# A hybrid attention, DeltaNet and MoE step: the 16x16 blocks of the DeltaNet scan turned on VectorE, planes in DRAM moved by half, triangles written by the sync queue

## Chip, cores and metric

The kernel runs on one core of a Trainium2 chip. The metric is the device time of one execution in microseconds. Three runs of the kernel before took 2502.2, 2504.52 and 2506.75 us: median 2504.52. Everything is float32.

## The reference

One trunk layer runs over 256 context tokens and 1024 latent tokens (D = 1024): a modulated input projection, two token mixers side by side (grouped-query attention, and a gated DeltaNet in both directions), their merge, and a hierarchical mixture of experts. The change touches the DeltaNet scan alone. For 8 heads of 64 channels, two directions and chunks of 64 tokens it computes

```python
lmat = jnp.where(strict, jnp.einsum('bhnik,bhnjk->bhnij', k_beta, k) * decay, 0.0)
tmat = lax.linalg.triangular_solve(eye + lmat, jnp.broadcast_to(eye, lmat.shape),
                                   left_side=True, lower=True, unit_diagonal=True)
u = jnp.einsum('bhnij,bhnjv->bhniv', tmat, v_beta)
w = jnp.einsum('bhnij,bhnjk->bhnik', tmat, k_beta * jnp.exp(g)[..., None])
intra = jnp.where(incl, jnp.einsum('bhnik,bhnjk->bhnij', q, k) * decay, 0.0)
def step(S, xs):                                   # one chunk after the other
    v_new = u_c - jnp.einsum('bhck,bhkv->bhcv', w_c, S)
    o_c = jnp.einsum('bhck,bhkv->bhcv', q_c, S) + jnp.einsum('bhij,bhjv->bhiv', a_c, v_new)
    S = S * jnp.exp(gl_c)[..., None, None] + jnp.einsum('bhck,bhcv->bhkv', k_c, v_new)
```

For every chunk, head and direction a unit triangular 64x64 matrix has to be inverted.

## The kernel before

The kernel is one program for five engines with hand-written semaphores; between its stages all engines meet. The fourth stage is the scan. There are 20 chunks, 4 of context and 16 of latent tokens. Iteration s handles chunk s of the forward direction together with the matching chunk of the backward direction, so 16 matrices of 64x64 at once. They lie on the 128 partitions as two halves (h) of 64 rows, with eight matrices side by side (a = 4 d + p: direction d, pair of heads p).

The engines run in their own order through the same loop, from s = -4 to 20 (AHEAD = 4). In iteration s they prepare chunk n = s + 4 (decays, Gram products, masked triangles la) and finish chunk s (inverse, new values, state, outputs).

The inverse is built in levels. First all 16x16 diagonal blocks are inverted by substitution, for two chunks at a time: 2 chunks x 16 matrices x 4 blocks = 128 blocks, one per partition. This is base(b) on VectorE for the chunks 2b and 2b+1, in iteration n = 2b + 2, an even s: rows 1 to 7 behind L1703, rows 8 to 15 at the end of the iteration behind L1726. Each row is a product (L1661) and a negated sum (L1664), each waited for before the next. The blocks are then doubled twice on TensorE with masks (the products x4, t4, u4 and x5, u5; the masks at L1678, the subtractions at L1701, L1703 and L1726 on VectorE).

To bring the blocks onto one partition each, and the inverses back into 64x64 planes, the data go through DRAM:

- GpSimd writes the triangle of chunk n - 1 from la to lt_scratch, one DMA per direction and half (L2039), behind its own work of the iteration.
- SP reads the diagonal blocks, one DMA per direction (L569), into b_turn (forward) and b_in (backward). Blocks of the backward direction are upper triangles, so ScalarE turns them (L1296) from b_in to b_turn.
- VectorE substitutes. The result is b_inv. Both the inverse and its transpose are needed; ScalarE turns all of it into b_invt (L1319), at the end of its iteration.
- SP writes b_inv and b_invt to tu_scratch (L551: two chunks x two directions x two forms, eight DMAs), waits until they have landed, and reads 64x64 planes into tu (L559: two chunks x two forms x two directions x two halves, sixteen DMAs). The parts off the diagonal blocks were zeroed once, at the start of the program. After that it reads the next blocks.

A plane in DRAM is 64x64 + 64 elements, so that consecutive diagonal blocks lie 16 x 64 + 16 elements apart over matrices and chunks alike.

On TensorE an iteration is: x4 (waits for tu and for the mask of the iteration before); the decay products (L923, L924); kv and av of chunk s - 1 (wait for ScalarE's copy L1280 of the new values); t4 (waits for L1678) and u4; two products with constants; x5; the product with the state; the Gram products (L953); u5; the product of the state with the queries; vn. All but L923, L924 and L953 are issued at L900: 32 small matmuls each, 16 matrices in two passes. On VectorE the order is: mask L1678, state L1698, L1701, L1703, outputs, base(b, 1, 8) if even, mask L1678, triangles L1722, L1726, base(b, 8, 16) if even. On ScalarE: L1280, eight exponentials L1285, L1290, the turn L1296, eight copies L1303, L1307, L1313, the turn L1319.

Of the kernel before, what the change touches and what calls it, by code (L numbers as in the profile page):

```python
# [22 lines left out]
P = 128  # L23
# [8 lines left out]
C = 64  # L32
# [13 lines left out]
def shape_constants():  # L46

    part, free = np.arange(P), np.arange(P)
    half, t = part // C, part % C
    same = (half[:, None] == half[None, :]).astype(np.float32)  # L50
    j = np.arange(C)
    upto = [t[:, None] <= j[None, :], t[:, None] >= j[None, :]]
    after_bd = [(t[:, None] > t[None, :]) * same, (t[:, None] < t[None, :]) * same]
    level = []
    for l in LEVELS:
        for d in range(2):
            b = 1 << l
# [11 lines left out]
    parts = [np.eye(P), same, np.ones((P, P))] + upto + after_bd + level + [eye, -eye, rot, before]  # L69
    return np.concatenate([np.asarray(a, np.float32) for a in parts], axis=1)  # L70
# [21 lines left out]
def build(nc, a, outs):  # L92
    ctx = ExitStack()
    with ctx:
# [21 lines left out]
        tu_d = nc.dram_tensor("tu_scratch", [4, 2, P, 16 * PLANE // P], F32).ap()  # L116
# [13 lines left out]
        eye_st, neg_eye, rot, before = take(C), take(C), take(P), take(P)  # L130
# [3 lines left out]
        def small_row(n):  # L134
# [49 lines left out]
          gm_ready decay_mm e_ready gr_ready e_masked el_ready kd_ready qd_ready gram_mm la_ready lt_out bt_in bt_turned  # L184
          base_done base_turned tu_out x4_mm x4_ready t4_mm t4_ready u4_mm u4_ready x5_mm x5_ready u5_mm u5_ready
# [151 lines left out]
        b_in, b_turn, b_inv, b_invt = [scr(256, "R1").rearrange("p (r c) -> p r c", r=16) for _ in range(4)]  # L337
# [17 lines left out]
        def planes_of(x, n, d, h):  # L355
            return bass.AP(x.tensor, (16 * n + 8 * d + 4 * h) * PLANE, [[C, C], [PLANE, 4], [1, C]])
# [91 lines left out]
        def _(sp):  # L448
# [86 lines left out]
            def blocks_of(x, n, d):  # L535
                return bass.AP(x.tensor, (16 * n + 8 * d) * PLANE, [[16 * C + 16, 32], [C, 16], [1, 16]])

            def block_rows(s, d):
                o = C * d + 32 * (s % 2)
                return slice(o, o + 32)  # L540
# [20 lines left out]
            for s in range(NCK):  # L561
                sp.wait_ge(S["lt_out"], 64 * (s + 1))
                if s % 2 == 0 and s > 0:
                    inverses_back(s // 2 - 1)
                if s // 2 > 0:
                    sp.wait_ge(S["base_done"], s // 2)
                    sp.wait_ge(S["bt_turned"], s // 2)
                for d in range(2):
                    sp.dma_start((b_turn, b_in)[d][block_rows(s, d)], blocks_of(lt_d, s, d)).then_inc(S["bt_in"], 16)  # L569
                if s == CTX_CH + 2:  # L570
# [4 lines left out]
            inverses_back(NCK // 2 - 1)  # L575
# [92 lines left out]
        def _(pe):  # L668
# [237 lines left out]
            for s in range(-AHEAD, NCK + 1):  # L906
# [5 lines left out]
                if now:  # L912
                    pe.wait_ge(S[f"tu_in{s % 3}"], landed(s, 3, 8))
# [208 lines left out]
        def _(act):  # L1122
# [152 lines left out]
            for s in range(-AHEAD, NCK + 1):  # L1275
# [15 lines left out]
                if n >= 2 and n % 2 == 0 and n // 2 - 1 < NCK // 2:  # L1291
                    b = n // 2 - 1
                    act.wait_ge(S["bt_in"], 64 * (b + 1))
                    if b > 0:
                        act.wait_ge(S["base_done"], b)
                    f(b_turn[C:2 * C].rearrange("p r c -> p c r"), b_in[C:2 * C], ACT.Copy).then_inc(S["bt_turned"], 1)  # L1296
# [17 lines left out]
                if n >= 2 and n % 2 == 0 and n // 2 - 1 < NCK // 2:  # L1314
                    b = n // 2 - 1
# [109 lines left out]
        def _(dve):  # L1425
# [233 lines left out]
            def substitute(b, i):  # L1659
# [3 lines left out]
                signal = "base_done" if i == 15 else "dve_chain"  # L1663
                v.tensor_reduce(b_inv[:, i, 0:i], tmp, AX.X, ALU.add, negate=True).then_inc(S[signal], 1)  # L1664
                dve.wait_ge(S[signal], count(signal))

            def base(b, first, end):
                if first == 1:
                    dve.wait_ge(S["bt_in"], 64 * (b + 1))
                    dve.wait_ge(S["bt_turned"], b + 1)  # L1670
                    if b > 0:
                        dve.wait_ge(S["base_turned"], b)
                        dve.wait_ge(S["tu_out"], 128 * b)
                for i in range(first, end):
                    substitute(b, i)

# [4 lines left out]
            for s in range(-AHEAD, NCK + 1):  # L1681
# [34 lines left out]
                if new:  # L1716
                    dve.wait_ge(S["gram_mm"], n + 1)
                    dve.wait_ge(S["e_masked"], n + 1)
                    if s > 0:
                        dve.wait_ge(S["av_mm"], s)  # L1720
                        dve.wait_ge(S["lt_out"], 64 * s)
# [230 lines left out]
        def _(pool):  # L1952
# [28 lines left out]
            for i in range(4):  # L1981
                for x in range(2):
                    pool.dma_start(tu_d[i, x], zero_f).then_inc(S["pool_dma"], 16)
# [40 lines left out]
            for s in range(-AHEAD, NCK):  # L2024
# [8 lines left out]
                if 1 <= n <= NCK:  # L2033
                    pool.wait_ge(S["la_ready"], n)
                    if n - 1 > 0:
                        pool.wait_ge(S["lt_out"], 64 * (n - 1))
                    for d in range(2):
                        for h in range(2):
                            pool.dma_start(planes_of(lt_d, n - 1, d, h), la[(n - 1) % RING][h * C:(h + 1) * C, 1, 4 * d:4 * d + 4]).then_inc(S["lt_out"], 16)  # L2039
# [77 lines left out]
```

## Time and profile before

| | before |
|---|---|
| median of three runs | 2504.52 us |
| the profiled execution | 2506.25 us |
| its span, first to last instruction | 2504.3 us |
| mean granted TensorE clock | 0.928 of full |
| TensorE busy (share of the span) | 2159.4 us (86%) |
| VectorE, ScalarE, GpSimd busy | 906.5, 682.8, 266.2 us |
| the scan in it | about 799 to 1236 us |

The span is about 2 us shorter than the time of the execution. The profile's page gives busy time by engine, the span in 40 slices, the chain that ended last and the costliest groups of instructions; a wait is written as the waiting instruction, an arrow and what ended the wait. The page's chain follows the end of the program and begins behind the scan, at 1326 us, so the scan has to be read from its own stretch: what ended the waits, and the engines' instructions in order of time. Numbers in brackets at the end of a line of the timeline are the idle time ahead of it and what ended it.

### The profile page before, as it was taken

Reading aid. Unit: us, or ns where it says so; the run is one execution under the profiler, and the core shown is the slowest. Engines: PE = TensorE matmul, PEld = TensorE weight load, DVE = VectorE, ACT = ScalarE, POOL = GpSimd, SP = SyncE. Lnnn points to the kernel's source line nnn. Section 1 sums busy time; section 2 is a strip of 40 time slices with the busy share of each in tenths; the row PEclk is TensorE's granted clock in tenths of the full one; section 3 lists DMA queues with packets and bytes.
Section 4 is the critical chain, followed back from the end, with each engine's and each line's share of the span. In section 5 each row is a group of like instructions: output and inputs, shape, how many; then the busy total and the mean of one; then the engine's idle time right before and its main releaser. Section 6 shows DMA issues by size and latency. Waiting matters only on the chain. (4 is left out here: it accounts for less than half of the span.)

```text
span 2504.3 us, 39485 instructions
## 1 busy us (share of the span) xinstructions
PE 2159.4 (86%) x16431; PEld 1329.9 (53%) x16431; DVE 906.5 (36%) x1760; ACT 682.8 (27%) x1386; POOL 266.2 (11%) x381
## 2 busy tenths in 40 slices
PE   4987999989997587888897999999999699799960
PEld 3545676665553477877753555555455444344420
DVE  3254666634883355455551011010223300000116
ACT  6122666643441232332220000000111122122223
POOL 2000000000000444433100000000000000000013
PEclk8998999999998698999898999999999699999985
DMA  9324000010100232323203111120313455776225
GB/s 331 130 88 121 4 4 1 2 43 26 30 0 1 43 63 46 62 43 58 57 0 92 26 34 43 25 67 1 136 60 117 150 185 179 250 239 214 85 101 201
DMA packets 240544, 210.12 MB, mean 84 GB/s; under 512 B 130348, under 2 KB 202352, under 8 KB 239728
## 3 DMA queue, kind: packets, MB, share of 16 engines
q1 hardware_dynamic: 223632, 152.93, 20.5%
q0 software_dynamic: 11696, 36.31, 4.9%
q10 hardware_dynamic: 5040, 18.35, 1.8%
q8 instruction: 133, 2.18, 0.4%
q14 instruction: 43, 0.35, 0.0%
HBM read 165.37 MB, written 42.01 MB: 83 GB/s over the span
## 5 line engine op out<-in xcount | busy, mean ns | idle before, releaser
L741 PE MATMUL ps<-R 128*128 128x512 f32 (+1 forms) x816 | 301.2, 530 | 11.3 <-SPq L525 8.4
L1008 PE MATMUL ps<-R 128*128 128x512 f32 (+1 forms) x768 | 286.1, 526 | 19.9 <-DMA R<-in_w_dn_br_dram 17.8
L1084 PE MATMUL ps<-R 128*128 x560 | 260.1, 619 | 25.7 <-SPq L653 22.5
L900 PE MATMUL ps<-R 64*64 64x64 f32 x5120 | 181.7, 230 | 67.8 <-ACT R L1280 30.5
L741 PEld LDWEIGHTS ps<-R 128*128 128x128 f32 x816 | 158.6, 195 | 150.7 <-issue 132.8
L1008 PEld LDWEIGHTS ps<-R 128*128 128x128 f32 x768 | 147.2, 192 | 152.3 <-issue 144.9
L900 PEld LDWEIGHTS ps<-R 64*64 64x64 f32 x5120 | 172.0, 145 | 87.4 <-ACT R L1280 37.4
L1084 PEld LDWEIGHTS ps<-R 128*128 128x128 f32 x560 | 110.7, 199 | 169.6 <-issue 169.6
L1753 DVE TENSOR_TENSOR R<-ps,R 128x512 f32<-128x512 f32 (+1 forms) x48 | 28.9, 603 | 394.1 <-ACT R L1353 393.3
L1920 DVE COPY R<-ps 128x256 f32<-128x256 f32 x35 | 14.9, 425 | 383.4 <-PE ps L1109 383.4
L2071 POOL DMA_INDIRECT R<-h_scratch,slot_i x35 | 33.0, 942 | 1124.6 <-DVE slot_i L1903 749.6
L1535 DVE TENSOR_SCALAR_CACHE_REDUCE R<-ps 128x512 f32<-128x512 f32 (+1 forms) x208 | 128.4, 666 | 59.9 <-PE ps L826 59.8
L1030 PE MATMUL ps<-R 128*128 128x512 f32 x320 | 142.2, 604 | 3.9 <-PEq L1017 3.9
L1010 PE MATMUL ps<-R 128*128 128x512 f32 (+1 forms) x384 | 145.3, 521 | 0.0
L1353 ACT ACTIVATE R<-ps 128x512 f32<-128x512 f32 (+1 forms) x48 | 25.2, 526 | 412.4 <-PE ps L1010 411.6
L1094 PE MATMUL ps<-R 128*128 x280 | 127.7, 599 | 1.5 <-DVE R L1920 1.3
L845 PEld LDWEIGHTS ps<-cst,R 128*128 128x128 f32 x800 | 86.4, 142 | 58.9 <-issue 48.2
L845 PE MATMUL ps<-cst,R 128*128 128x128 f32 x800 | 105.0, 279 | 5.7 <-ACT R L1239 2.9
L826 PE MATMUL ps<-R 64*128 64x512 f32 (+1 forms) x416 | 106.5, 616 | 3.5 <-SPq L509 3.3
L1229 ACT ACTIVATE R<-R 128x1536 f32<-128x1536 f32 (+1 forms) x80 | 108.6, 1358 | 3.0 <-DVE R L1544 2.9
L1010 PEld LDWEIGHTS ps<-R 128*128 128x128 f32 x384 | 73.0, 190 | 64.5 <-issue 61.2
L1030 PEld LDWEIGHTS ps<-R 128*128 128x128 f32 x320 | 61.2, 194 | 78.6 <-issue 73.9
(265 smaller groups left out, 2700.0 us busy)
## 6 DMA issues: line engine op xcount, KB each, us to landing
R<-in_w_mod_dram SPq DMA_DIRECT2D x12, 2048.0 KB, 9.1
slot_output<-R ACTq DMA_DIRECT2D x35, 512.0 KB, 3.6
R<-in_w_gate_e_dram SPq DMA_DIRECT2D x16, 1024.0 KB, 6.8
R<-in_w_up_e_dram SPq DMA_DIRECT2D x16, 1024.0 KB, 10.2
R<-in_w_down_e_dram SPq DMA_DIRECT2D x16, 1024.0 KB, 12.0
R<-in_w_in_dram SPq DMA_DIRECT2D x30, 512.0 KB, 5.4
R<-tu_scratch SPq DMA_DIRECT2D x160, 64.0 KB, 2.6
R<-in_x_sample_dram SPq DMA_DIRECT2D x16, 512.0 KB, 6.0
```

The costliest lines, as they stand in the source:

```text
L741: last = mm(ps[:, u % 4, 0:w], w_sb[n % NW][:, k, :], hT[:, k, c0:c0 + w], start=(k == 0), stop=(k == KD - 1))
L826: last = mm(ps[:, 2 * (u % 2) + g, 0:w], qT[lo, h4, qt * P:(qt + 1) * P], kT[lo, c0 + j * 512:c0 + j * 512 + w], start=True, stop=True)
L845: last = turn128(ps[:, 4 + v % 3, k * P:(k + 1) * P], s_sb[i % 2][g][:, j * 512 + k * P:j * 512 + (k + 1) * P], ident)
L900: last = mm(ps[lo, bank, a * C:(a + 1) * C], lhs(a)[lo], rhs(a)[lo], start=start and (alone or a == 0), stop=stop and (alone or a == PAIRS ...
L1008: mm(ps[:, o + x, 0:w], wk[:, x, k, :], hT[:, k, c0:c0 + w], start=(k == 0), stop=(k == KD - 1))
L1010: last = mm(ps[:, o + 2 + x, 0:w], wb[:, x, k, :], (aoT, odT)[x][:, k, c0:c0 + w], start=(k == 0), stop=(k == 3))
L1030: last = mm(ps[:, 2 * (n % 2) + h, :], mT[:, k, n * P:(n + 1) * P], ow[k][:, h * 512:(h + 1) * 512], start=(k == 0), stop=(k == KD - 1))
L1084: last = mm(ps[:, 2 + t % 2, :], hsT[t % 2][:, k, :], R[:, bass.ds(at + (RB + k * 512), 512)], start=(k == 0), stop=(k == KD - 1))
L1094: last = mm(ps[:, 5 + u % 3, :], hidT[t % 2][:, k, :], R[:, bass.ds(at + (RB + 4096 + k * D + h * 512), 512)], start=(k == 0), stop=(k == 1))
L1229: f(s_sb[i % 2][g][:, 0:w], s_sb[i % 2][g][:, 0:w], ACT.Exp, bias=shift[i % 2][g], accum_out=sums[qt % 2][:, g, h4:h4 + 1]).then_inc(S["p_ ...
L1535: v.tensor_scalar(s_sb[i % 2][g][:, j * 512:j * 512 + w], ps[:, 2 * (u % 2) + g, 0:w], HD ** -0.5, None, ALU.mult, ALU.max, accum_out=tops ...
L2071: pool.indirect_dma_start(hs[t % 2], None, h2_d, bass.IndirectOffsetOnAxis(ap=slot_i[:, t:t + 1], axis=0)).then_inc(S[f"hs_in{t % 2}"], 16)
```

## The change

It does five things.

1. Planes in DRAM are addressed by half, not by direction and half: planes_of takes eight planes at once. A chunk's inverses come back in four DMAs, a pair's in eight. blocks_of covers the blocks of two chunks on 128 partitions: one DMA reads them all into b_in, and one per form writes them. The order of tu_scratch changes to form first, then chunk, so that two chunks lie side by side.
2. With this order the direction of a block is bit 4 of its partition. A constant of two columns, block_dir, holds 1 for one direction and 0 for the other. VectorE makes b_turn as b_in times one mask plus turned b_in times the other, and after the substitution b_t and b_u in the same way from b_inv: six instructions per pair.
3. ScalarE's two turns and their semaphores are gone. base_done is now signalled by the last of the new instructions.
4. b_t uses the memory of b_in.
5. GpSimd's writes of the triangles are gone. SP does them, two DMAs per chunk, as soon as the triangle is ready: the one of an odd chunk after the loads of the pair before, the one of an even chunk after the read of the blocks and before the inverses are waited for.

```diff
-        def planes_of(x, n, d, h):
-            return bass.AP(x.tensor, (16 * n + 8 * d + 4 * h) * PLANE, [[C, C], [PLANE, 4], [1, C]])
+        def planes_of(x, n, h):
+            return bass.AP(x.tensor, (16 * n + 8 * h) * PLANE, [[C, C], [PLANE, 8], [1, C]])
+
+        def blocks_of(x, n):
+            return bass.AP(x.tensor, 16 * n * PLANE, [[16 * C + 16, P], [C, 16], [1, 16]])
...
             def inverses_back(b):
                 sp.wait_ge(S["base_done"], b + 1)
-                sp.wait_ge(S["base_turned"], b + 1)
                 for s in (2 * b, 2 * b + 1):
                     if s - 4 >= 0:
-                        sp.wait_ge(S[f"tu_in{(s - 4) % 3}"], landed(s - 4, 3, 8))
-                    for d in range(2):
-                        for x in range(2):
-                            src = b_inv if x == d else b_invt
-                            sp.dma_start(blocks_of(tu_d, 2 * (s % 4) + x, d), src[block_rows(s, d)]).then_inc(S["tu_out"], 16)
-                sp.wait_ge(S["tu_out"], 128 * (b + 1))
+                        sp.wait_ge(S[f"tu_in{(s - 4) % 3}"], landed(s - 4, 3, 4))
+                for x, src in enumerate((b_t, b_u)):
+                    sp.dma_start(blocks_of(tu_d, 4 * x + 2 * (b % 2)), src).then_inc(S["tu_out"], 16)
+                sp.wait_ge(S["tu_out"], 32 * (b + 1))
                 for s in (2 * b, 2 * b + 1):
                     if s - 2 > 0:
                         sp.wait_ge(S["vn_mm"], s - 2)
                     for x in range(2):
-                        for d in range(2):
-                            for h in range(2):
-                                sp.dma_start(tu[s % 3][h * C:(h + 1) * C, x, 4 * d:4 * d + 4], planes_of(tu_d, 2 * (s % 4) + x, d, h)).then_inc(S[f"tu_in{s % 3}"], 16)
...
+                        for h in range(2):
+                            sp.dma_start(tu[s % 3][h * C:(h + 1) * C, x], planes_of(tu_d, 4 * x + s % 4, h)).then_inc(S[f"tu_in{s % 3}"], 16)
+
+            def triangles_out(n):
+                sp.wait_ge(S["la_ready"], n + 1)
+                if n > 0:
+                    sp.wait_ge(S["lt_out"], 32 * n)
+                for h in range(2):
+                    sp.dma_start(planes_of(lt_d, n, h), la[n % RING][h * C:(h + 1) * C, 1]).then_inc(S["lt_out"], 16)
+
+            triangles_out(0)
+            for b in range(NCK // 2):
+                triangles_out(2 * b + 1)
+                sp.wait_ge(S["lt_out"], 64 * (b + 1))
+                if b > 0:
+                    sp.wait_ge(S["base_done"], b)
+                sp.dma_start(b_in, blocks_of(lt_d, 2 * b)).then_inc(S["bt_in"], 16)
+                if 2 * b + 2 < NCK:
+                    triangles_out(2 * b + 2)
+                inverses_back(b)
...
             def base(b, first, end):
                 if first == 1:
-                    dve.wait_ge(S["bt_in"], 64 * (b + 1))
-                    dve.wait_ge(S["bt_turned"], b + 1)
-                    if b > 0:
-                        dve.wait_ge(S["base_turned"], b)
-                        dve.wait_ge(S["tu_out"], 128 * b)
+                    dve.wait_ge(S["bt_in"], 16 * (b + 1))
+                    v.tensor_scalar(b_turn, b_in, block_dir[:, 0:1], None, ALU.mult).then_inc(S["dve_chain"], 1)
+                    dve.wait_ge(S["dve_chain"], count("dve_chain"))
+                    v.scalar_tensor_tensor(b_turn, b_in.rearrange("p r c -> p c r"), block_dir[:, 1:2], b_turn, ALU.mult, ALU.add).then_inc(S["dve_chain"], 1)
+                    dve.wait_ge(S["dve_chain"], count("dve_chain"))
                 for i in range(first, end):
                     substitute(b, i)
+                if end == 16:
+                    if b > 0:
+                        dve.wait_ge(S["tu_out"], 32 * b)
+                    for x, dst in enumerate((b_t, b_u)):
+                        v.tensor_scalar(dst, b_inv, block_dir[:, x:x + 1], None, ALU.mult).then_inc(S["dve_chain"], 1)
+                        dve.wait_ge(S["dve_chain"], count("dve_chain"))
+                        signal = "base_done" if x else "dve_chain"
+                        v.scalar_tensor_tensor(dst, b_inv.rearrange("p r c -> p c r"), block_dir[:, 1 - x:2 - x], dst, ALU.mult, ALU.add).then_inc(S[signal], 1)
+                        dve.wait_ge(S[signal], count(signal))
...
-                if n >= 2 and n % 2 == 0 and n // 2 - 1 < NCK // 2:
-                    b = n // 2 - 1
-                    act.wait_ge(S["base_done"], b + 1)
-                    if b > 0:
-                        act.wait_ge(S["tu_out"], 128 * b)
-                    f(b_invt.rearrange("p r c -> p c r"), b_inv, ACT.Copy).then_inc(S["base_turned"], 1)
...
-                if 1 <= n <= NCK:
-                    pool.wait_ge(S["la_ready"], n)
-                    if n - 1 > 0:
-                        pool.wait_ge(S["lt_out"], 64 * (n - 1))
-                    for d in range(2):
-                        for h in range(2):
-                            pool.dma_start(planes_of(lt_d, n - 1, d, h), la[(n - 1) % RING][h * C:(h + 1) * C, 1, 4 * d:4 * d + 4]).then_inc(S["lt_out"], 16)
```

## Rows read from the trace of the kernel before

**Rows 1.** Waits, 800 to 1245 us: waiter <- releaser, total us, times, longest.
```profile
ACT R L1319 <- DVE R L1664: 98.9, 10, 10.6
...
PE ps L900 <- ACT R L1280: 30.5, 10, 3.6
...
PE ps L900 <- DMA R<-tu_scratch: 21.7, 9, 8.3
```

**Rows 2.** Timeline of TensorE in the scan: start, length (us), instructions, [idle before <- releaser].
```profile
859.22 1.97 PE L900 MATMUL ps<-R 64*64 64x64 f32 x32 [8.27 <-DMA R<-tu_scratch]
...
1079.87 5.45 PE L900 MATMUL ps<-R 64*64 64x64 f32 x128 [3.61 <-ACT R L1280]
...
1095.76 1.15 PE L900 MATMUL ps<-R 64*64 64x64 f32 x32 [1.88 <-DMA R<-tu_scratch]
...
1100.45 3.95 PE L900 MATMUL ps<-R 64*64 64x64 f32 x128
...
1109.71 1.10 PE L900 MATMUL ps<-R 64*64 64x64 f32 x32
...
1119.22 3.95 PE L900 MATMUL ps<-R 64*64 64x64 f32 x128 [3.41 <-ACT R L1280]
...
1209.46 4.88 PE L900 MATMUL ps<-R 64*64 64x64 f32 x160 [1.15 <-DMA R<-tu_scratch]
```

**Rows 3.** Two stretches behind idle ones; the last numbers: PEclk, DMA share, GB/s.
```profile
1079.87:1085.20 5.33, 5.33 (x130) 5.33 (x132) 2.31 (x9) 2.17 (x9) 1.58 (x3) 0.68 0.48 52
...
1095.76:1098.70 2.94, 2.94 (x37) 2.51 (x37) 0.69 (x1) 0.00 (x0) 2.04 (x4) 0.69 0.78 176
```

**Rows 4.** Timeline of VectorE, even iteration: substitution from first to last, masks.
```profile
1105.20 0.16 DVE L1661 TENSOR_TENSOR R<-R 128x1 f32<-128x1 f32 x1
...
1108.25 0.69 DVE L1678 TENSOR_TENSOR R<-ps,cst 128x512 f32<-128x512 f32 x1
...
1111.07 0.68 DVE L1726 TENSOR_TENSOR R<-R,ps 128x512 f32<-128x512 f32 x1
...
1117.68 0.39 DVE L1664 TENSOR_REDUCE R<-R 128x15 f32<-128x225 f32 x1
```

**Rows 5.** Timeline of ScalarE: the turn of the blocks read.
```profile
1104.47 0.64 ACT L1296 ACTIVATE R<-R 64x256 f32<-64x256 f32 x1 [0.57 <-DMA R<-lt_scratch]
```

**Rows 6.** Timeline of SP's queue for one pair: start, length of all issues together.
```profile
1079.53 4.03 SPq L551 DMA_DIRECT2D tu_scratch<-R  x8
1086.73 12.55 SPq L559 DMA_DIRECT2D R<-tu_scratch  x16
1099.37 2.14 SPq L569 DMA_DIRECT2D R<-lt_scratch  x4
```

**Rows 7.** Groups of VectorE by form, whole span: count, busy us, mean ns.
```profile
L1621 DVE SCALAR_TENSOR_TENSOR R<-R,prm 128x256 f32<-128x256 f32 x24 | 11.6, 485 | 0.9
...
L1661 DVE TENSOR_TENSOR R<-R 128x225 f32<-128x225 f32 x10 | 5.4, 545 | 0.3
L1661 DVE TENSOR_TENSOR R<-R 128x81 f32<-128x81 f32 x10 | 5.1, 514 | 0.3
...
L1617 DVE TENSOR_SCALAR R<-R,prm 128x256 f32<-128x256 f32 x12 | 4.2, 353 | 87.3 <-ACT R L1183 87.3
```

**Rows 8.** Timeline of GpSimd at the end of the even iteration.
```profile
1111.84 1.48 POOL L2020 TENSOR_TENSOR R<-R 128x256 f32<-128x256 f32 x2 [2.20 <-PE ps L900]
...
1114.64 2.54 POOL L2039 DMA_DIRECT2D lt_scratch<-R  x4
1120.87 1.27 POOL L2043 TENSOR_TENSOR R<-R,cst 128x512 f32<-128x512 f32 x1 [3.69 <-ACT R L1285]
```

**Rows 9.** DMA issues on the page: count, KB each, median us from issue to landing.
```profile
lt_scratch<-R POOLq DMA_DIRECT2D x80, 64.0 KB, 2.2
...
tu_scratch<-R SPq DMA_DIRECT2D x80, 32.0 KB, 1.9
```

**Rows 10.** SP's loads of weights by line: ns of one issue, least/median/most.
```profile
L479 SPq DMA_DIRECT2D R<-in_w_in_dram x13: 368/388/4446, 33.1 to 676.1; - x13
```

More of the change, by code:

```diff
@@ L68, in shape_constants @@
     before = (part[:, None] < free[None, :]).astype(np.float32)
-    parts = [np.eye(P), same, np.ones((P, P))] + upto + after_bd + level + [eye, -eye, rot, before]
+    parts = [np.eye(P), same, np.ones((P, P))] + upto + after_bd + level + [eye, -eye, rot, before, (part[:, None] // 16) % 2 == np.arange(2)[None, :]]
     return np.concatenate([np.asarray(a, np.float32) for a in parts], axis=1)
@@ L115, in build @@
         lt_d = nc.dram_tensor("lt_scratch", [T // C, 16 * PLANE], F32).ap()
-        tu_d = nc.dram_tensor("tu_scratch", [4, 2, P, 16 * PLANE // P], F32).ap()
+        tu_d = nc.dram_tensor("tu_scratch", [2, 4, P, 16 * PLANE // P], F32).ap()
         cst = sb("cst", [P, const_np.shape[1]])
@@ L129, in build @@
         levels = take(2 * 2 * C).rearrange("p (l d c) -> p l d c", l=2, d=2)
-        eye_st, neg_eye, rot, before = take(C), take(C), take(P), take(P)
+        eye_st, neg_eye, rot, before, block_dir = take(C), take(C), take(P), take(P), take(2)
         small = sb("small", [P, small_np.shape[1]])
@@ L336, in build @@
         kd, qd, kdec, rv = [by_head(scr(512, "R1")) for _ in range(4)]
-        b_in, b_turn, b_inv, b_invt = [scr(256, "R1").rearrange("p (r c) -> p r c", r=16) for _ in range(4)]
+        b_in, b_turn, b_inv, b_u = [scr(256, "R1").rearrange("p (r c) -> p r c", r=16) for _ in range(4)]
+        b_t = b_in
         b_tmp = scr(256, "R1")
@@ L556, in inverses_back @@
                     for x in range(2):
-                        for d in range(2):
-                            for h in range(2):
-                                sp.dma_start(tu[s % 3][h * C:(h + 1) * C, x, 4 * d:4 * d + 4], planes_of(tu_d, 2 * (s % 4) + x, d, h)).then_inc(S[f"tu_in{s % 3}"], 16)
[L561 to L567, printed above, removed]
-                for d in range(2):
-                    sp.dma_start((b_turn, b_in)[d][block_rows(s, d)], blocks_of(lt_d, s, d)).then_inc(S["bt_in"], 16)
-                if s == CTX_CH + 2:
+                        for h in range(2):
[16 more added lines that the diff above has]
+                inverses_back(b)
+                if b == CTX_CH:
                     sp.wait_ge(S["s_ready"], PAIRS * CTX_CH)
@@ L912, in _ @@
                 if now:
[L913 removed]
+                    pe.wait_ge(S[f"tu_in{s % 3}"], landed(s, 3, 4))
                     pe.wait_ge(S["la_ready"], s + 1)
@@ L1662, in substitute @@
                 dve.wait_ge(S["dve_chain"], count("dve_chain"))
-                signal = "base_done" if i == 15 else "dve_chain"
-                v.tensor_reduce(b_inv[:, i, 0:i], tmp, AX.X, ALU.add, negate=True).then_inc(S[signal], 1)
-                dve.wait_ge(S[signal], count(signal))
+                v.tensor_reduce(b_inv[:, i, 0:i], tmp, AX.X, ALU.add, negate=True).then_inc(S["dve_chain"], 1)
+                dve.wait_ge(S["dve_chain"], count("dve_chain"))
             def base(b, first, end):
                 if first == 1:
-                    dve.wait_ge(S["bt_in"], 64 * (b + 1))
-                    dve.wait_ge(S["bt_turned"], b + 1)
-                    if b > 0:
-                        dve.wait_ge(S["base_turned"], b)
-                        dve.wait_ge(S["tu_out"], 128 * b)
+                    dve.wait_ge(S["bt_in"], 16 * (b + 1))
[3 more added lines that the diff above has]
+                    dve.wait_ge(S["dve_chain"], count("dve_chain"))
                 for i in range(first, end):
                     substitute(b, i)
+                if end == 16:
[3 more added lines that the diff above has]
+                        v.tensor_scalar(dst, b_inv, block_dir[:, x:x + 1], None, ALU.mult).then_inc(S["dve_chain"], 1)
+                        dve.wait_ge(S["dve_chain"], count("dve_chain"))
+                        signal = "base_done" if x else "dve_chain"
+                        v.scalar_tensor_tensor(dst, b_inv.rearrange("p r c -> p c r"), block_dir[:, 1 - x:2 - x], dst, ALU.mult, ALU.add).then_inc(S[signal], 1)
+                        dve.wait_ge(S[signal], count(signal))
             def masked(out, bank, level):
```

20 lines of the change are left out of this document (4 added, 16 removed).

## Prediction

> **What bounds the kernel now.** The change touches only the DeltaNet scan, so I first read the list of waits of that stretch. TensorE is idle there 30.5 us until ScalarE at L1280 and 21.7 us until a load out of tu_scratch; ScalarE stands 98.9 us at L1319 until VectorE's last reduction L1664 [rows 1]. Then I read the scan in order of time. It repeats every two chunks (a pair), because the 16x16 blocks of two chunks are inverted together; I call the iteration with that work even, the next one odd.
>
> TensorE's own work at full clock: from 1100.45 (the product kv of the even iteration) to 1119.22 - 3.41 = 1115.81 (kv of the odd one could start) it has no idle [rows 2]. That is one iteration, 15.36 us, so a pair is 30.7. But from 1079.87 to 1119.22 a pair lasts 39.35 us, and from the first x4 product at 859.22 to the one at 1209.46 nine pairs take 350.2 us, 38.9 each [rows 2]. The 8.2 us above 30.7 are 3.4 to 3.6 us idle until ScalarE, some 2 us until tu_scratch, and the clock: behind an idle stretch the granted clock is 0.68 and 0.69, a mean of time at 1.2 and at 2.4 GHz [rows 3], and four products take 5.45 us, against 3.95 at full clock [rows 2].
>
> There is a second way to count the same pair, around the loop blocks, inverses, loads, next blocks: VectorE 1105.20 to 1118.07 = 12.9 us with both parts of the substitution [rows 4]; ScalarE's turn back 0.65 (the length of its turn in, [rows 5]); SP's eight writes and their landing 1079.53 to 1086.73 = 7.2; sixteen loads 12.6; four reads of lt_scratch and their landing 1099.37 to 1104.47 = 5.1 [rows 5, 6]; ScalarE's turn in 0.65. Sum 39.1 us. So this loop sets the pace, not TensorE, and TensorE's idle changes its name from pair to pair because all hangs on the loop.
>
> **The change part by part.**
> Taken from ScalarE: two turns, 0.65 each on the loop. More: at L1319 ScalarE waited for the whole substitution, and the copy L1280, queued behind it, feeds TensorE. That wait goes, and L1280 can run when its product is done. What is late next is VectorE itself: L1678, for which TensorE's t4 product waits, stands behind the substitution.
>
> Added to VectorE: one masked tensor_scalar and one masked scalar_tensor_tensor with a turned operand in front, and two such couples behind. The nearest forms, 128x256 from SBUF with a per-partition scalar, are 353 ns at L1617 and 485 ns at L1621 [rows 7]; with gaps of 0.03 a couple is 0.90. In front 0.9, behind 1.8, 2.7 us a pair; nothing excuses it, each instruction has 256 elements to read, so this is the low end. Above: the turned read. L1661 reads turned and takes 545 ns for 225 elements, more than L1621 for 256 [rows 7]: 0.15 more per couple, 3.2. I take 2.7. The front 0.9 hides: L1678, now 1108.25 to 1108.94, would end at 1109.8, and TensorE comes to u5, which needs it, at 1109.71 [rows 2, 4]. If that cover fails it costs 0.9 a pair. The 1.8 behind does not hide.
>
> A collision: L1661 takes 514 ns for 81 elements, nearly what it takes for 225 [rows 7]; the 81 runs at 1112.2, beside GpSimd's product of 1111.84 [rows 8]. With ScalarE free earlier, GpSimd's mask L2043 (1.27 us, now released by ScalarE at 1120.87 [rows 8]) moves to where the new VectorE instructions stand. I add 0.3. The Trainium skill, "SBUF — State Buffer", practical consequences, speaks against the change here: a VectorE instruction in a two-port mode, as a tensor_scalar within SBUF can be, and a GpSimd instruction exclude one another for their whole length. No row here shows a tensor_scalar beside GpSimd; its outcome is rival B.
>
> TensorE's idle in a pair: let E be the end of L1726 in the even iteration, 1111.75 [rows 4]. TensorE then has vn, x4 and decay until 1115.81 and kv, av, half of 3.95: 6.0 us, now without the stop for L1280. VectorE has 6.3 of substitution (1111.75 to 1118.07), 1.8 new, 0.3 of collision and 0.7 for L1678: t4 may start at E + 9.2. Idle 3.2 us. Before, TensorE went on at E + 7.5 with kv and av at the low clock (half of 5.45), and t4 came at E + 10.2. So of the 3.4 us that the wait row promises only 1.0 comes in at this place; VectorE takes over the rest of the wait. A pair by TensorE: 30.7 + 3.2 + 1.0 for the clock (5.45 - 3.95 = 1.5 now; less, because the idle comes later and TensorE works until just before it) = 34.9.
>
> SP's transfers. Writes of inverses go from eight to two, each of 2,048 runs of 64 B instead of 512. Low: 2 x 0.5 (4.03 / 8 now [rows 6]) and a landing of 1.9 [rows 9] = 2.9; high: as now, 7.2. The DMA engines are 0.48 busy for 5.33 us over them [rows 3], 2.6 us, and that stays: 1.9 + 2.6 = 4.5. Loads go from sixteen to eight, of double size. Low 8 x 0.5 = 4.0; high 12.6 as now. L479 issues DMAs of 1,024 runs in 0.39 us [rows 10], so the issue does not go by the number of runs; but 176 GB/s at a share of 0.78 [rows 3] is 226 GB/s, and the 1 MB needs 4.7 us. I take 6.0. The next chunk's inverses then arrive 4.5 + 0.1 + four loads 3.0 + 2.7 landing (now TensorE goes 2.7 us behind the eighth of the sixteen, 1086.73 + 8 x 0.78) = 10.3 us behind the first write, now 1095.76 - 1079.53 = 16.2. TensorE wants them at about E + 20; the first write is at E + 8.5, so this wait goes too.
>
> Moved past SP: the writes of the triangles. GpSimd issued four per chunk in 2.54 us [rows 8], beside everything else. Of SP's two per chunk, those of an even chunk stand free; those of the odd chunk are queued behind the eight loads, and the read of blocks and TensorE's inverses of the pair after wait for that: 2 x 0.64 + 2.2 landing [rows 8, 9] = 3.5 us more in the loop; 3.2 if issued in 0.5 each, 4.8 if the issue doubles with the size. The read of blocks, once instead of four times: 0.5 + 2.9 landing = 3.4 against 5.1. GpSimd gains 5 us a pair, worth nothing: TensorE's idle does not name it [rows 1].
>
> The loop then: VectorE 12.9 + 2.7 - 0.9 (taken by its present wait for the Gram product) = 14.7, writes 4.5, loads 6.0, triangles 3.5, blocks 3.4, five hand-overs at 0.1: 32.6 us. That is below TensorE's 34.9, and 34.9 stands.
>
> **Sum.** Nine pairs: 9 x (38.9 - 34.9) = 36 us. Start: TensorE waits 8.27 us for the first inverses [rows 2]; their way gets shorter by 16.2 - 10.3 and ScalarE's 0.65, and VectorE's part longer by 1.8: 4.8. Together 41. Nothing outside the scan is touched; two more columns of constants count as nothing, loaded before the first products. The profiled execution took 2506.25 us with a span of 2504.3; 2506.25 - 41 = 2465. The median of the runs is 1.7 lower: 2464.
>
> **Rivals.**
> B, VectorE costs more: tensor_scalars wait out GpSimd's 1.27 us about twice a pair. 2.5 more per pair, 37.4: 9 x 1.5 + 3 = 16, 2488. For it: the 81-element row; against: most couples fall where GpSimd is idle. 15%.
> C, slower: a DMA on SP is priced by its runs and bytes, not by its number. Writes 7.2, loads 12.6, triangles 4.8, blocks 4.4, hand-overs 0.5, VectorE 15.7: 45 us a pair; 9 x 6.1 + 3 = 58, 2562. It decides from where SP's part passes 38.9 - 14.7 - 0.5 = 23.7 us (I have 17.4): what GpSimd did beside the loop would then stand in it. Against it: L479. 10%.
> D, the clock holds through the shorter idle and transfers take their low ends: 33.2 a pair, 9 x 5.7 + 5.5 = 57, 2447. 13%.
> S, the change does not do what it says: waits are only renamed, since the VectorE work that ended them grows, and the pair keeps its 38.9 but for half a microsecond: within 0.2%, about what a measurement of this kernel can tell. 4%.
> Mine: 58%.
>
> **How the numbers follow.** 2464 is the likeliest case. The low end is 2440, below D, the high end 2495, past B. Outside are S, C and slivers of D and B: some 18%. Faster by over 0.2% are mine, B and D, 0.86; within, S, 0.04; slower, C, 0.10.
>
> **What would show it.** In the profile after: TensorE's idle until L1280 is gone; in its place some 3 us until L1678 once a pair, ahead of the t4 product. Each couple on VectorE takes near 0.9 us. SP comes from its first write of inverses to its first load in 4.5 us and issues eight loads in 5 to 6.5. VectorE waits under 1 us for lt_scratch. From the first x4 product to that of the tenth pair pass about 314 us, now 350. I am wrong if the loads still take 10 us (C), if VectorE's added work passes 4 us a pair (B), or if VectorE waits for the blocks in every pair: then the loop through SP is still the bound.

## The result and the profile after

The changed kernel takes 2481.55 us (median of five runs, 2473.98 to 2484.83) where the kernel before takes 2502.87 (five runs, 2501.73 to 2506.75): ratio 0.9908, 95% interval 0.9892 to 0.9925. It is faster, by 21 us; 2464 was forecast, with a range of 2440 to 2495. The profiled execution took 2483.28 us, span 2481.4: 23 us below the profiled one of before, 41 had been worked out. So the sign and the range held, and nearly half of the gain is missing.

First the waits of the scan, after: waiter <- releaser, total us, times, longest. They answer [rows 1].

```profile
ACT R L1280 <- PE ps L900: 85.0, 20, 5.6
...
PE ps L900 <- DVE R L1674: 44.0, 18, 5.4
...
PE ps L900 <- DMA R<-tu_scratch: 10.3, 1, 10.3
...
DVE R L1657 <- DMA R<-lt_scratch: 6.2, 1, 6.2
```

TensorE no longer waits for ScalarE's copy (but for 0.7 us ahead of the scan's last products), and for tu_scratch once only, at the start. In their place stand 44.0 us until VectorE's mask (L1674, which was L1678): nine waits ahead of t4, 36.2 us together, and nine ahead of u5, 7.8. VectorE waits for its blocks once, at the start. That is the picture that was forecast. The sizes are in the timeline of TensorE over one pair (start, length in us, [idle before <- releaser]), against [rows 2]:

```profile
854.79 1.97 PE L900 MATMUL ps<-R 64*64 64x64 f32 x32 [10.27 <-DMA R<-tu_scratch]
...
1065.58 3.68 PE L900 MATMUL ps<-R 64*64 64x64 f32 x64 [3.84 <-DVE R L1674]
1069.05 3.11 PE L900 MATMUL ps<-cst,R 64*64 64x64 f32 x64
1072.00 1.10 PE L900 MATMUL ps<-R 64*64 64x64 f32 x32
...
1085.41 2.03 PE L900 MATMUL ps<-cst,R 64*64 64x64 f32 x64
...
1091.29 1.15 PE L900 MATMUL ps<-R 64*64 64x64 f32 x32 [0.23 <-DVE R L1674]
...
1103.10 3.68 PE L900 MATMUL ps<-R 64*64 64x64 f32 x64 [3.86 <-DVE R L1674]
```

A pair goes from 1065.58 to 1103.10, 37.52 us. It holds an idle of 3.86 and four products at a low clock, 1065.58 to 1072.00 = 6.42 us, where the same four at full clock take 3.8 (two take 1085.41 to the next product at 1087.28, 1.87). In the nine pairs these four take 5.27 to 6.43 us, 52.3 in all, 18.3 above full clock; this pair is one of the dear ones. From the first x4 product at 854.79 to that of the tenth pair at 1187.1 nine pairs take 332 us, 36.9 each; before it was 38.9, forecast 34.9. The granted clock in these stretches (the last numbers are PEclk, DMA share and GB/s; of the columns before, PE is the first):

```profile
1062.00:1065.50 3.50, 0.00 (x0) 0.00 (x0) 3.33 (x7) 0.00 (x0) 1.23 (x3) 0.87 0.00 0
1065.58:1069.00 3.42, 3.42 (x64) 3.42 (x66) 2.16 (x9) 0.60 (x1) 0.00 (x0) 0.50 0.69 80
1069.00:1072.00 3.00, 3.00 (x71) 3.00 (x68) 0.69 (x1) 0.98 (x5) 0.00 (x0) 0.60 0.02 1
1072.00:1077.00 5.00, 5.00 (x150) 5.00 (x148) 1.86 (x3) 1.91 (x7) 1.41 (x2) 1.00 0.74 165
```

In this pair the clock falls to 1.2 GHz near the end of the idle stretch and comes back to 2.4 GHz only after some 6 us of products. In [rows 3] the mean over the first 5.33 us was 0.68; here 0.50 over 3.42 us and 0.60 over 3.00. So it goes in six of the nine pairs. In the three others (t4 at 916.75, 954.30 and 1141.74) the whole idle stretch is at full clock, and it falls about 1 us after TensorE has taken up work again. One of them, its t4 row and two stretches:

```profile
916.75 2.83 PE L900 MATMUL ps<-R 64*64 64x64 f32 x64 [3.85 <-DVE R L1674]
```

```profile
913.00:916.70 3.70, 0.00 (x0) 0.00 (x0) 3.52 (x7) 0.00 (x0) 1.39 (x3) 1.00 0.00 0
918.00:921.00 3.00, 3.00 (x62) 3.00 (x60) 2.18 (x6) 0.60 (x1) 0.00 (x0) 0.50 0.46 55
```

VectorE at the end of the even iteration, after (the same columns), as [rows 4]:

```profile
1061.81 0.39 DVE L1651 TENSOR_REDUCE R<-R 128x15 f32<-128x225 f32 x1
1062.24 0.82 DVE L1667 TENSOR_SCALAR R<-R,cst 128x256 f32<-128x256 f32 x1
1063.10 0.64 DVE L1670 SCALAR_TENSOR_TENSOR R<-R,cst 128x256 f32<-128x256 f32 x1
1063.77 0.35 DVE L1667 TENSOR_SCALAR R<-R,cst 128x256 f32<-128x256 f32 x1
1064.16 0.64 DVE L1670 SCALAR_TENSOR_TENSOR R<-R,cst 128x256 f32<-128x256 f32 x1
1064.84 0.69 DVE L1674 TENSOR_TENSOR R<-ps,cst 128x512 f32<-128x512 f32 x1
```

GpSimd beside it, after, as [rows 8]:

```profile
1061.59 1.32 POOL L2032 TENSOR_TENSOR R<-R,cst 128x512 f32<-128x512 f32 x1 [2.77 <-ACT R L1285]
```

SP's queue for the pair, after, as [rows 6]:

```profile
1064.83 1.37 SPq L545 DMA_DIRECT2D tu_scratch<-R  x2
1070.60 5.98 SPq L552 DMA_DIRECT2D R<-tu_scratch  x8
1077.08 2.29 SPq L559 DMA_DIRECT2D lt_scratch<-R  x2
1081.25 0.37 SPq L567 DMA_DIRECT2D R<-lt_scratch  x1
```

The four turning instructions and their gaps last from 1062.20 to 1064.80, 2.6 us; 2.1 were forecast with the collision. SP's part came nearly as worked out: writes until the first load 5.8 here and 4.6 in most pairs (forecast 4.6), loads 6.0 (6.0).

### The profile page after: what moved, and what is told of

It is laid out like the page before. It is cut to its first block and busy times, and to the rows that moved or that the text cites. A ratio compares the mean times of both kernels' runs of the same rounds, so it can differ in the third digit from the quotient of the medians.

```text
span 2481.4 us, 39269 instructions
## 1 busy us (share of the span) xinstructions
PE 2155.5 (87%) x16431; PEld 1329.5 (54%) x16431; DVE 943.3 (38%) x1820; ACT 673.1 (27%) x1366; POOL 217.0 (9%) x301
## 5 line engine op out<-in xcount | busy, mean ns | idle before, releaser
L1916 DVE COPY R<-ps 128x256 f32<-128x256 f32 x35 | 14.9, 424 | 383.4 <-PE ps L1109 383.4
## 6 DMA issues: line engine op xcount, KB each, us to landing
R<-in_w_up_e_dram SPq DMA_DIRECT2D x16, 1024.0 KB, 10.1
```

## The experiments

Each was timed beside the kernel before on the same chip: 2504.36 us for the first four, 2500.55 for the last four. The changed kernel's 2481.55 stands beside 2502.87; differences to it of under 5 us are not read. Parts of the program that no edit touches also differ a little between the profiled executions, so the scan alone is given too, from the start of its first decay product to the start of its last products (kv and av of the last chunk):

| | scan, us | against the changed kernel |
|---|---|---|
| before | 431.4 | +23.9 |
| changed | 407.5 | |
| warm | 399.0 | -8.5 |
| no_back | 371.2 | -36.3 |
| mask_first | 401.1 | -6.5 |
| loads_split | 460.9 | +53.4 |
| gpsimd_lt | 417.6 | +10.1 |
| before_turn_late | 439.8 | +32.3 |
| kt_first | 404.5 | -3.1 |
| best | 389.9 | -17.6 |

**What do the idle stretch and its clock cost?** Four dummy products ahead of t4:

```diff
+                if now and s % 2 == 1 and s < NCK - 1:
+                    pe.wait_ge(S["u4_ready"], s)
+                    for _ in range(4):
+                        product(4, feature(s, 1), lambda a: eye_st)
                 if now:
                     pe.wait_ge(S["x4_ready"], s + 1)
```

> The changed kernel, with four dummy products of TensorE (into a PSUM bank that is free then) ahead of the t4 product in each odd iteration, so that TensorE works through the 3.85 us in which it waits for VectorE's mask. Theory (my sum failed at the clock: the idle drops it to half for some 5.6 us, and six products take 6.4 us instead of 3.8): the t4 product starts when it did, the two slow rows of 3.68 and 3.11 us become 1.9 each, 2.6 us less per pair, nine pairs: 23 us less than the changed kernel, about 2458. Rival (the slow products come from something else, such as the loads of inverses that land then): no gain, or up to 5 us more if the dummies end late.

Measured 2470.84 us (2466.88 to 2479.69), ratio 0.9872 (0.9839 to 0.9906). Adding work made it 11 us faster: the rival falls. A pair of its TensorE timeline, and below it a row of its list of waits:

```profile
1057.55 3.90 PE L900 MATMUL ps<-cst,R 64*64 64x64 f32 x128
1061.59 2.08 PE L900 MATMUL ps<-R 64*64 64x64 f32 x64
...
1092.85 3.90 PE L900 MATMUL ps<-cst,R 64*64 64x64 f32 x128
1096.90 2.08 PE L900 MATMUL ps<-R 64*64 64x64 f32 x64 [0.15 <-DVE R L1678]
```

```profile
DVE R L1661 <- DMA R<-lt_scratch: 10.6, 5, 6.0
```

The slow rows are gone (2.08 instead of 3.68), and this pair lasts 1096.90 - 1061.59 = 35.3 us. But only half of the expected 23 us came. The 23 took the 2.6 us of the pair shown for all nine, and over the nine the clock costs 18.3. Of those 18.3 us a part comes back as waiting: TensorE's idle ahead of u5 is 13.4 us here and 7.8 in the changed kernel, it waits 2.0 us for tu_scratch behind the start, and VectorE waits for its blocks in four more pairs, 4.6 us together. Over six pairs (the u5 product, 906.35 to 1121.55) the mean is 35.9, in the changed kernel 37.5 (904.95 to 1129.94); over all nine, from the first x4 product to that of the tenth pair, 36.0 against 36.9.

**What does VectorE's work behind the substitution cost?** Without the four instructions; b_inv goes out for both forms, so where a transpose was due the inverse is wrong. VectorE's wait for the inverses of the pair before (tu_out) moves ahead of the substitution, since that now writes what SP reads:

```diff
-                    for x, dst in enumerate((b_t, b_u)):
-                        v.tensor_scalar(dst, b_inv, block_dir[:, x:x + 1], None, ALU.mult).then_inc(S["dve_chain"], 1)
...
-                        v.scalar_tensor_tensor(dst, b_inv.rearrange("p r c -> p c r"), block_dir[:, 1 - x:2 - x], dst, ALU.mult, ALU.add).then_inc(S[signal], 1)
...
-                for x, src in enumerate((b_t, b_u)):
+                for x, src in enumerate((b_inv, b_inv)):
```

> The changed kernel without the four instructions that turn the result of the substitution (the result goes out as it is for both forms, so the inverses are wrong where a transpose was due): the price of VectorE's added work behind the substitution. Theory (VectorE is what TensorE waits for, and the idle costs clock): 2.6 us a pair from the instructions, and up to 2.6 from the clock since 1.2 us of idle remain: 23 to 45 us less than the changed kernel, 2437 to 2459. Rival (the loop through SP is nearly as long): no more than the 2.1 us a pair that VectorE has to spare now before it needs the blocks: 2462 to 2465.

Measured 2442.38 us (2434.05 to 2446.28), ratio 0.975 (0.9718 to 0.9782): 39 us below the changed kernel, as the theory wants, not 17 to 20 as the rival. The instructions are 2.6 us a pair, 23 in nine. The other 16 us are near the 18.3 that the clock costs the changed kernel: here every t4 row is at full clock. The idle before t4 in its timeline; a pair and all nine as one stretch each (PEclk is 1.00 and 0.99); and the nine of the changed kernel (0.93):

```profile
1009.38 2.08 PE L900 MATMUL ps<-R 64*64 64x64 f32 x64 [1.24 <-DVE R L1668]
```

```profile
980.00:1013.99 33.99, 30.89 (x852) 28.50 (x850) 22.30 (x60) 11.65 (x43) 11.46 (x18) 1.00 0.37 69
857.00:1150.00 293.00, 267.73 (x7418) 248.81 (x7418) 200.24 (x543) 95.70 (x344) 94.98 (x148) 0.99 0.34 62
```

```profile
860.00:1187.00 327.00, 282.51 (x7417) 264.05 (x7418) 221.47 (x579) 95.11 (x343) 94.32 (x147) 0.93 0.30 56
```

**Same work, other order.** VectorE's x4 mask is placed between the last row and the four turning instructions:

```diff
                 if end == 16:
+                    if early and s + 1 >= 0:
+                        x4_mask(s + 1)
                     if b > 0:
                         dve.wait_ge(S["tu_out"], 32 * b)
...
-                if now:
-                    dve.wait_ge(S["x4_mm"], s + 1)
...
+                if now and not (s % 2 == 1 and s < NCK - 1):
+                    x4_mask(s)
```

> The changed kernel, with VectorE's x4 mask of the next iteration placed between the last row of the substitution and the four instructions that turn the result. Same work. Theory: TensorE's t4 starts 2.6 us earlier, but the inverses go out 0.7 us later, and they land 12.0 us behind VectorE's last turn with about 2 us to spare before the change of order; so TensorE waits about 1.5 us for tu_scratch instead, and 1 to 1.5 us a pair remain, 9 to 14 us: 2467 to 2473. Rival (VectorE alone sets the pace and the transfers have room): 2.6 a pair and the clock time too, 25 to 40 us: 2442 to 2457.

Measured 2474.48 us (2473.53 to 2479.16), ratio 0.989 (0.9864 to 0.9915). Of 2.6 us a pair some 0.8 remain; the theory wanted 1 to 1.5 (2467 to 2473), so it is missed by little, and the rival's 2442 to 2457 by far. TensorE's idle before t4 shrank to 1.25, and it waits for tu_scratch in its place, in the pair shown with a slow product behind it (1.62 us, else 1.15). Timeline, and a row of its waits:

```profile
1055.71 2.08 PE L900 MATMUL ps<-R 64*64 64x64 f32 x64 [1.25 <-DVE R L1684]
...
1069.08 1.62 PE L900 MATMUL ps<-R 64*64 64x64 f32 x32 [1.86 <-DMA R<-tu_scratch]
```

```profile
PE ps L900 <- DMA R<-tu_scratch: 21.6, 10, 9.5
```

**Was the halving of the loads needed?** The planes come back in sixteen DMAs of four:

```diff
                         for h in range(2):
-                            sp.dma_start(tu[s % 3][h * C:(h + 1) * C, x], planes_of(tu_d, 4 * x + s % 4, h)).then_inc(S[f"tu_in{s % 3}"], 16)
+                            for d in range(2):
+                                sp.dma_start(tu[s % 3][h * C:(h + 1) * C, x, 4 * d:4 * d + 4], four_planes_of(tu_d, 4 * x + s % 4, h, d)).then_inc(S[f"tu_in{s % 3}"], 16)
```

> The changed kernel with one part undone: the 64x64 planes come back in sixteen DMAs of four planes, not in eight of eight. Theory (a load's price on SP is by its number; sixteen take 12.5 us, eight take 5.9): the write of the odd chunk's triangles waits for them 6 us longer, VectorE gets its blocks about 4 us late in each pair, and TensorE waits for inverses: 3 to 5 us a pair, 27 to 45 us more, 2508 to 2526, slower than the kernel before. Rival (the halving was not needed, the loads have room): within 5 us of the changed kernel.

Measured 2525.51 us (2514.06 to 2533.11), ratio 1.0076 (1.0051 to 1.0101): slower than the kernel before, 44 us above the changed one. The sixteen loads take 12.72 us, and the triangles stand behind them; VectorE waits for its blocks in every pair. SP's queue, and a row of its waits:

```profile
1061.60 12.72 SPq L556 DMA_DIRECT2D R<-tu_scratch  x16
1074.42 1.27 SPq L563 DMA_DIRECT2D lt_scratch<-R  x2
```

```profile
DVE R L1661 <- DMA R<-lt_scratch: 43.0, 10, 7.2
```

So these loads are priced by their number: eight of 512 runs take 6.0 us, sixteen of 256 runs, with the same bytes, 12.7. And the triangles on SP need the halved loads: without the halving the change loses. (The halved loads do not need the triangles on SP, as the next run shows.) It is the slow outcome that rival C described, reached by another way.

**What did the move of the triangles cost?** They go back to GpSimd:

```diff
-            triangles_out(0)
...
+                if 1 <= n <= NCK:
+                    pool.wait_ge(S["la_ready"], n)
+                    if n - 1 > 0:
+                        pool.wait_ge(S["lt_out"], 32 * (n - 1))
+                    for h in range(2):
+                        pool.dma_start(planes_of(lt_d, n - 1, h), la[(n - 1) % RING][h * C:(h + 1) * C, 1]).then_inc(S["lt_out"], 16)
```

> The changed kernel with the writes of the triangles back on GpSimd (two DMAs per chunk, by half), where they stood before. My prediction priced the move to SP at 3.5 us more in the loop. Theory now: SP's queue is free when the triangles are ready (they leave 0.03 us behind VectorE's instruction), while GpSimd first does its product and its decays and sends them some 3 us later; VectorE's blocks have 2.1 us to spare, so GpSimd's version is about 1 us a pair slower: 2482 to 2495. Rival (the prediction's reading, SP pays for them): 10 to 30 us faster than the changed kernel, 2452 to 2472.

Measured 2491.55 us (2486.95 to 2501.07), ratio 0.9967 (0.9952 to 0.9981): about 10 us slower than the changed kernel and still faster than the kernel before. The prediction's 3.5 us in the loop for this move had the wrong sign. GpSimd sends the triangles behind two other steps, and VectorE waits 16.3 us in eight pairs for its blocks, against 6.2 once. In the pair shown GpSimd also stops between the two DMAs, which it does in no other; why is open (timeline of GpSimd):

```profile
1081.48 1.42 POOL L2012 TENSOR_TENSOR R<-R 128x256 f32<-128x256 f32 x2 [2.20 <-PE ps L896]
1082.86 1.19 POOL L2007 TENSOR_TENSOR R<-cst,bg_st 128x256 f32<-128x256 f32 x2
1083.98 0.73 POOL L2030 DMA_DIRECT2D lt_scratch<-R  x1
1087.24 0.70 POOL L2030 DMA_DIRECT2D lt_scratch<-R  x1 [2.53 <-issue]
```

The triangles were ready at 1080.8 (the end of VectorE's L1714) and left at 1083.98 and 1087.24; in most pairs of this run both leave together, 3.2 us behind the triangles of the odd chunk; in the changed kernel, in the pair shown above, they leave 0.03 us behind. The Trainium skill ("DMA: Bandwidth & Descriptors", issuing engines are not separate DMA queues) says that DMAs of all engines run on the same 16 engines and that another issuer saves sequencer time only. Here the other issuer cost 10 us, and what the rows show of it is when it comes to the DMA in its order.

**Was the wait for ScalarE worth its row?** In the kernel before, the turn L1319 is moved behind the copy L1280:

```diff
                 if old:
                     act.wait_ge(S["vn_mm"], s)
                     f(rv, bank8(5), ACT.Copy).then_inc(S["vn_ready"], 1)
+                if n >= 3 and n % 2 == 1 and (n - 1) // 2 - 1 < NCK // 2:
+                    b = (n - 1) // 2 - 1
+                    act.wait_ge(S["base_done"], b + 1)
+                    if b > 0:
+                        act.wait_ge(S["tu_out"], 128 * b)
+                    f(b_invt.rearrange("p r c -> p c r"), b_inv, ACT.Copy).then_inc(S["base_turned"], 1)
...
-                if n >= 2 and n % 2 == 0 and n // 2 - 1 < NCK // 2:
```

> The kernel before, with ScalarE's turn of the inverse moved behind its next copy L1280, so that the copy no longer waits for the substitution; nothing else is changed. It takes away the wait that the list of waits puts at 30.5 us. Theory (the loop through SP sets the pace, that wait was only where it showed): within 5 us of the kernel before, 2499 to 2509, and TensorE's idle turns up until VectorE and until tu_scratch. Rival (the wait row is worth its face value): 25 to 35 us less, 2469 to 2479.

Measured 2508.17 us (2498.05 to 2516.86) against 2500.55: ratio 1.0034 (1.0014 to 1.0054). The 30.5 us of [rows 1] are gone, and the kernel is not faster, if anything slower. The turn is not late by the edit: it starts at 1082.80, and VectorE's last reduction ends at 1082.77. TensorE's idle until tu_scratch went from 21.7 to 54.1 us. Its timeline, and the row of its waits:

```profile
1083.54 2.08 PE L900 MATMUL ps<-R 64*64 64x64 f32 x64 [1.06 <-DVE R L1678]
1100.10 1.97 PE L900 MATMUL ps<-R 64*64 64x64 f32 x32 [5.93 <-DMA R<-tu_scratch]
```

```profile
PE ps L900 <- DMA R<-tu_scratch: 54.1, 10, 8.3
```

This bears out the prediction's reading of the kernel before: the loop through VectorE, ScalarE and SP set the pace.

**A product ahead of t4** that doesn't depend on VectorE:

```diff
+                if now:
+                    product(5, feature(s, 1), lambda a: eye_st).then_inc(S["kt_mm"], 1)
                     pe.wait_ge(S["x4_ready"], s + 1)
```

> The changed kernel with one product that does not depend on VectorE (the turn of k, 0.93 us) moved ahead of the t4 product. Same work. Theory (TensorE's idle until the mask is what counts): 0.93 us less in each of nine pairs and perhaps a little clock, 8 to 12 us less than the changed kernel, about 2472. Rival (the loop through SP has no room): within 3 us of it.

Measured 2477.37 us (2473.62 to 2481.97), ratio 0.9911 (0.9884 to 0.9938), between the two and not to be told from the changed kernel. The rows show why: the idle before t4 fell from 3.85 to 2.92, and the one before u5 in the even iteration rose from 0.23 to 1.41. There too VectorE is the later one, by now, with the new instructions ahead of the rows.

```profile
1087.08 1.15 PE L900 MATMUL ps<-R 64*64 64x64 f32 x32 [1.41 <-DVE R L1674]
1098.88 3.00 PE L900 MATMUL ps<-R 64*64 64x64 f32 x64 [2.92 <-DVE R L1674]
```

**Both loops shortened.** The mask first, the product first, and the inverses sooner: the first form is written when it is turned, and x4 waits only for the two loads of the form that it reads.

```diff
+                sp.wait_ge(S["diag_ready"], 2 * NT + b + 1)
+                sp.dma_start(blocks_of(tu_d, 2 * (b % 2)), b_t).then_inc(S["tu_out"], 16)
                 sp.wait_ge(S["base_done"], b + 1)
+                sp.dma_start(blocks_of(tu_d, 4 + 2 * (b % 2)), b_u).then_inc(S["wmod_in3"], 16)
...
-                    pe.wait_ge(S[f"tu_in{s % 3}"], landed(s, 3, 4))
+                    pe.wait_ge(S[f"tu_in{s % 3}"], landed(s, 3, 2))
```

(The two semaphores are ones that an earlier stage has done with, counted on from where it left them.)

> The changed kernel with four re-orderings, the same work: the x4 mask ahead of VectorE's four turning instructions, the turn of k ahead of t4, the first form of the inverse written as soon as it is turned, and TensorE's x4 product waiting only for the loads of the form that it reads. Theory (two loops of nearly the same length, so both have to be shortened): TensorE's idle until the mask is under 0.5 us, the inverses come 2 us sooner than in the version with the mask alone, the clock stays full; 33.5 to 34.5 us a pair against 37.2: 2447 to 2458. Rival (the loop through SP stays, whatever is done on VectorE and TensorE): no better than the mask alone, 2470 to 2478.

Measured 2456.1 us (2450.88 to 2458.53), ratio 0.9817 (0.9794 to 0.984): faster than both kernels, with the same work as the changed one; 18 of the 25 us to the changed kernel lie in the scan by the table, the rest where nothing differs. The gain came at the low end of what was expected: a pair lasts 35.5 us (u5, 900.42 to 1113.26, six pairs), not 34. Its timeline, and a row of its waits:

```profile
1053.00 2.08 PE L902 MATMUL ps<-R 64*64 64x64 f32 x64 [0.33 <-DVE R L1688]
1056.68 1.15 PE L902 MATMUL ps<-cst,R 64*64 64x64 f32 x32 [1.60 <-DVE S_lat L1705]
...
1078.12 1.15 PE L902 MATMUL ps<-R 64*64 64x64 f32 x32 [1.40 <-DVE R L1688]
```

```profile
PE ps L902 <- DMA R<-tu_scratch: 6.9, 1, 6.9
```

TensorE waits for tu_scratch at the start only. What is left, 0.33, 1.60 and 1.40 us a pair, is all until VectorE, in three places.

## Why the prediction was right in sign and short in size

*What bounds the kernel: right.* The loop through SP set the pace, and removing the wait row alone gives nothing (before_turn_late).

*What is late next: right.* TensorE's wait for L1280 went over to the mask behind VectorE's substitution: forecast some 3 us once a pair, measured 3.85, and 36.2 in nine against 28.8.

*The clock: this term failed.* The prediction took 1.0 us a pair, "less, because the idle comes later and TensorE works until just before it". It is 6.42 - 3.8 = 2.6 in the pair shown and 2.0 in the mean of nine (18.3), so 9 us are missing here. That reason was wrong: in six pairs the clock falls inside the stretch all the same, and in the three others 1 us behind it, at nearly the same price (5.33 us for the four products). The stretch did not shrink either, 3.85 us against 3.4 to 3.6 before and 3.2 forecast. The dummy products show that the slow rows hang on the stretch, not on the loads that land then. The length of the stretch does not fix the price: in [rows 2] the idle of 3.41 us ahead of 1119.22 left the four products at 3.95, full clock, and that of 3.61 ahead of 1079.87 did not; the prediction took its 1.5 from the second alone. In the changed kernel none of the nine pairs goes free.

*VectorE's instructions behind: 2.6 instead of 1.8 + 0.3.* A turned scalar_tensor_tensor takes 0.64 to 0.66, not 0.485; the prediction had this price, 0.15 more for each, and left it out of the sum. The first tensor_scalar takes 0.82 and the second 0.35: that is the collision with GpSimd, 0.47 a pair, not 0.3. It ends at 1063.06, 0.15 us behind GpSimd's mask. That distance is the same wherever in the mask it starts, here 0.65 us into it and in a pair of mask_first, a run above, 0.06 us into it:

```profile
1020.01 1.35 DVE L1677 TENSOR_SCALAR R<-R,cst 128x256 f32<-128x256 f32 x1
```

```profile
1019.95 1.26 POOL L2039 TENSOR_TENSOR R<-R,cst 128x512 f32<-128x512 f32 x1 [3.21 <-ACT R L1285]
```

So 1.35 us at the worst, ending at 1021.36, again 0.15 behind. The Trainium skill's rule ("SBUF — State Buffer", practical consequences) that the two exclude one another for the whole length of the first is borne out by this. It happened once in most pairs, not twice, and for its last half only: rival B's 2.5 us is out, though the measured 2481.55 lies nearer to B's 2488 than to 2464.

*The front couple: put at nothing, and not quite nothing.* TensorE's idle ahead of u5 is 0.22 to 0.24 us in five of nine pairs, but 0.87, 1.35, 1.35 and 3.09 in the others, 7.8 in all. The kernel before had such waits too (14.9 us in five, until L1678), which neither [rows 1] nor the prediction lists. And the slack is all used, as kt_first shows.

*Transfers.* Writes, loads and blocks came as worked out, and rival C falls by loads_split's other side: the price goes by the number of DMAs. The triangles' 3.5 us in the loop were wrong: the prediction queued them behind the loads, but in the pair shown the loads end (1076.58) before the triangles are ready (1077.05), and they leave at once. In three of nine pairs they leave 0.1 us behind the last load and waited for it, 8.7 us in the first of them and under 1 in the two others; on the whole SP sends them sooner than GpSimd, whose price the prediction had put at nothing. As SP's loop was not the longer one, the error did not enter the sum.

*The sum.* In the pair shown: idle 3.86 against 3.2, clock 2.6 against 1.0, the rest 27.2 against 26.9 (27.24 from 1072.00 to 1099.24, and 30.7 less the 3.8 of the four products): 34.9 + 0.7 + 1.6 + 0.3 = 37.5, as measured. Over nine pairs 314.1 were forecast and 332.3 measured: 7.4 more idle ahead of t4, 7.8 ahead of u5, 9.3 more for the clock, and 6.3 less for the rest, mostly since the ninth pair prepares no new chunk, which the forecast did not take off. So the errors partly cancel, and that part is luck. Nine pairs give 9 x (38.9 - 36.9) = 18 us. For the start 4.8 were forecast; the first x4 product comes 859.22 - 854.79 = 4.4 sooner, although the scan itself starts later, its first decay product at 803.57 and not at 801.65: within the scan it is 6.3.

What stays open: what decides when the granted clock falls, from 1 us before the products to 1 us after their start for the same 3.85 us of idle, and when it comes back, 3 to 6 us after their start.

## What to carry to other kernels

A wait row names who came last, not what it is worth: count the loop that the work goes round, and take the wait away to see whether the time moves. Where an idle stretch of TensorE is renamed, not removed, and gets longer, price its clock again from the rows behind it; here the clock cost 18 us in nine pairs and the instructions 23. When two loops are nearly equally long, shorten both: of the order changes alone the mask gave 7 us and the product nothing clear of the noise; both, with the sooner inverses, gave 25.

## What the runs showed of the hardware

- Around idle stretches of 3.85 us (nine pairs) the granted clock fell to 1.2 GHz, inside them in some and 1 us behind them in others, and four products of 3.8 us took 5.3 to 6.4; stretches of 1.25 us (no_back, mask_first) left it at 2.4 GHz. Between, the kernel before has stretches of 3.4 us with either outcome. Filling the stretch with products that nobody reads saved 11 us of 2481.
- A float32 tensor_scalar of 128x256 within SBUF takes 0.35 us alone. Started beside a GpSimd product of 128x512 that reads SBUF, it ended 0.15 us behind that product wherever it had started: 0.62, 0.82, 1.08 and 1.35 us long. In the last 0.06 us of such a product it took 0.34 (mask_first, at 1055.58).
- A scalar_tensor_tensor with a turned 16x16 operand (steps of 64 bytes) takes 0.65 us for 256 elements, against 0.485 for the form with plain rows [rows 7].
- One DMA of 2,048 runs of 64 bytes is issued by SP in 0.37 us when the queue is free, two in 1.3; eight loads of 512 runs in 5.3 to 6.4, sixteen of 256 in 12.7.
